# HGRN2's output norm on one Trainium2 core: 1/sqrt by logarithm and exponential on ScalarE in place of square roots and reciprocals

## The reference

```
def rmsnorm(x, g):
    xf = x.astype(jnp.float32)
    y = xf * lax.rsqrt(jnp.mean(xf * xf, axis=-1, keepdims=True) + RMS_EPS)
    return (y * g.astype(jnp.float32)).astype(x.dtype)
...
hg_o = hgrn2_chunked(qq, kk, g, vv)
hg_o = rmsnorm(hg_o, hg_norm_g).reshape(b, s, HG_VAL_WIDTH).astype(x.dtype)
u_hg = jnp.einsum('bse,ed->bsd', hg_o * jax.nn.silu(hg_z), w_hg_proj)
```

## Time and profile before

| | us |
|---|---|
| median of 3 runs (1442.77 to 1444.6) | 1443.66 |
| the profiled execution, its own time | 1442.67 |
| its span, first to last instruction | 1440.6 |
| TensorE matmuls busy | 1355.1 (94%) |
| VectorE busy | 959.2 (67%) |
| GpSimd busy | 709.6 (49%) |
| ScalarE busy | 577.1 (40%) |

### The profile page before, as it was taken

One profiled execution on the slowest core, in us unless ns is written; L12 is line 12 of the kernel. 1 busy time (PEld: TensorE's weight loads), 2 busy tenths in 40 slices (PEclk: granted clock), 3 DMA queues, 4 the chain that ended last, 5 costly groups with the idle time before them and its releaser, 6 DMA issues.

```text
span 1440.6 us, 23216 instructions
## 1 busy us (share of the span) xinstructions
PE 1355.1 (94%) x8408; PEld 1122.2 (78%) x8408; DVE 959.2 (67%) x1074; ACT 577.1 (40%) x958; POOL 709.6 (49%) x488
## 2 busy tenths in 40 slices
PE   5689999999999999999999999999898979999998
PEld 4568778778878878878878887887776768888886
DVE  4827976976977886896797697687533275545323
ACT  8336255346335535634634634543423321111131
POOL 6655744654565554564574465555556522223210
PEclk8799999999999999999999999999989989999999
DMA  5121121112111121121112111122343475433512
GB/s 147 29 74 30 60 86 32 61 45 71 62 30 59 46 74 59 30 89 59 30 61 73 45 61 45 58 74 89 103 158 105 151 241 177 154 95 116 192 44 102
DMA packets 134348, 119.41 MB, mean 83 GB/s; under 512 B 10096, under 2 KB 116592, under 8 KB 134256
## 3 DMA queue, kind: packets, MB, share of 16 engines
q1 hardware_dynamic: 125040, 92.84, 20.5%
q10 hardware_dynamic: 9216, 25.17, 5.1%
HBM read 88.63 MB, written 29.36 MB: 82 GB/s over the span
## 4 chain that ended last, share of the span: by engine, by line
PE 66%; DVE 12%; issue 9%; ACT 4%; POOL 4%; DMA 4%; SPq 0%; DVEq 0%; POOLq 0%; ACTq 0%
PE banks L1506 32%; PE banks L1756 12%; PE banks L1778 6%; PE banks L1584 4%; PE banks L1563 3%; DMA w_raw<-in_w_in 3%; DVE hk L1040 3%; PE banks L1574 2%; POOL b_lo L568 2%; POOL b_sum L568 2%; DVE forget L1040 1%; DVE hq L1040 1%; DVE scT L1272 1%; PE banks L1643 1%; DVE scT L1244 1%
## 5 line engine op out<-in xcount | busy, mean ns | idle before, releaser
L1506 PE MATMUL banks<-a_hi,b_hi 128*128 128x512 f32 x1120 | 468.4, 418 | 37.7 <-POOL b_lo L568 17.4
L1506 PE MATMUL banks<-a_hi,b_lo 128*128 128x512 f32 x1120 | 445.5, 398 | 0.0
L1506 PE MATMUL banks<-a_lo,b_hi 128*128 128x512 f32 x1120 | 444.5, 397 | 0.0
L568 POOL TENSOR_TENSOR b_lo<-w_raw,b_hi 128x512 fp32r<-128x512 f32 x120 | 183.0, 1533 | 300.8 <-ACT b_hi L656 291.7
L1506 PEld LDWEIGHTS banks<-a_hi,b_hi 128*128 128x128 f32 x1120 | 215.3, 192 | 86.2 <-POOL b_lo L568 19.9
L1506 PEld LDWEIGHTS banks<-a_hi,b_lo 128*128 128x128 f32 x1120 | 214.3, 191 | 48.1
L1506 PEld LDWEIGHTS banks<-a_lo,b_hi 128*128 128x128 f32 x1120 | 215.7, 193 | 37.5
L568 POOL TENSOR_TENSOR b_lo<-b_sum,b_hi 128x512 fp32r<-128x512 f32 x120 | 176.8, 1474 | 129.1 <-ACT b_hi L656 129.1
L1142 DVE TENSOR_TENSOR_SCAN kappa<-kappa 128x128 f32<-128x128 f32 (+3 forms) x64 | 97.0, 1516 | 100.8 <-ACT kappa L773 100.8
L656 ACT ACTIVATE b_hi<-b_sum 128x512 fp32r<-128x512 f32 x120 | 75.5, 631 | 136.9 <-POOL b_sum L568 136.9
L640 POOL TENSOR_TENSOR w_lo<-w_raw,w_hi 128x1024 fp32r<-128x1024 f32 x20 | 48.1, 2409 | 153.7 <-ACT w_hi L656 153.7
(11 more groups left out here) (194 smaller groups left out, 2467.7 us busy)
## 6 DMA issues: line engine op xcount, KB each, us to landing
w_raw<-in_w_in SPq DMA_DIRECT2D x80, 512.0 KB, 5.0
gate_d<-gate_out SPq DMA_DIRECT2D x16, 512.0 KB, 3.6
gate_in<-gate_d ACTq DMA_DIRECT2D x32, 256.0 KB, 2.9
x_tok<-in_x SPq DMA_DIRECT2D x8, 512.0 KB, 6.1
z_d<-z_out SPq DMA_DIRECT2D x8, 512.0 KB, 2.7
hz_d<-z_out SPq DMA_DIRECT2D x8, 512.0 KB, 2.7
osb_d<-o_sb SPq DMA_DIRECT2D x8, 512.0 KB, 5.7
ohg_d<-hq SPq DMA_DIRECT2D x8, 512.0 KB, 2.7
```

The lines of the kernel that those rows point to most:

```text
L568: return nc.gpsimd.tensor_tensor(dst, a, b, op)
L1506: last = mm(bank, w[:, s, k, :], t[s][:, k, :], start=opens and k == 0 and z == 0, stop=k == QUAD - 1 and z == 2, skip_group_check=not opens)
```

## The change

The square roots become logarithms, `log(mean + eps)`, still by halves; one exponential of the whole tile with the scale -0.5 gives `scT` = 1/sqrt; the four reciprocals and their semaphore go; `normalize` waits for the exponential, and the transposes of `turn_in` wait for the logarithms, which are now what reads `attended`.

```diff
-        def quarter(t, i):
-            return t[:, i * S // 4:(i + 1) * S // 4]
...
                 if u == 12:
                     act.wait_ge(hn_done, a + 1)
                     for b in range(2):
-                        nc.scalar.activation(halfs(scT, b), (turned, attended)[b], ACT.Sqrt, bias=EPS).then_inc(rms_done, 1)
+                        nc.scalar.activation(halfs(scT, b), (turned, attended)[b], ACT.Ln, bias=EPS).then_inc(log_done, 1)
+                    act.wait_ge(log_done, 2 * a + 2)
+                    nc.scalar.activation(scT[:, :], scT[:, :], ACT.Exp, scale=-0.5).then_inc(rms_done, 1)
...
-            def invert(a, i):
-                dve.wait_ge(rms_done, 2 * a + i // 2 + 1)
-                v.reciprocal(quarter(scT, i), quarter(scT, i)).then_inc(recip_done, 1)
-
             def normalize(a):
-                dve.wait_ge(recip_done, 4 * a + 4)
+                dve.wait_ge(rms_done, a + 1)
                 dve.wait_ge(on_done, 2 * a + 2)
                 tt(hq[:, :], hq[:, :], scT[:, :], ALU.mult).then_inc(hg_norm, 1)
...
                 take_c12(pairs[1], n + 1)
-                if attend:
-                    for i in range(3):
-                        invert(a, i)
                 take_c21(pairs[1], n + 1, h)
-                if attend:
-                    invert(a, 3)
...
             take_c12(GATE_PAIR, n)
-            for i in range(3):
-                invert(a, i)
             dve.wait_ge(gate_stored[0], 16)
             take_c21(GATE_PAIR, n)
-            invert(a, 3)
             normalize(a)
...
-                    need(pe, rms_done, 2 * h)
+                    need(pe, log_done, 2 * h)
```

More of the change, by code:

```diff
@@ L328, in build @@
         hn_done = sem("hn_done")
+        log_done = sem("log_done")
         rms_done = sem("rms_done")
-        recip_done = sem("recip_done")
         hg_norm = sem("hg_norm")
```

## The result

| | before | after |
|---|---|---|
| median, us | 1443.31 (16 runs, 1440.47 to 1444.9) | 1447.18 (16 runs, 1444.65 to 1449.03) |
| the profiled execution, its own time, us | 1442.67 | 1447.67 |
| its span, us | 1440.6 | 1445.9 |

The ratio is 1.0027 with a 95% interval of 1.0019 to 1.0034: slower by 3.9 us. The forecast was 1447.6, slower too.

A forecast was written before the change was run, and what follows sets the result against it. TensorE, busy 94% of the span, was taken to bound the kernel. Seven heads at +1.0 us (+7.0) and the gate stretch (-3.1) gave +3.9 on 1443.66, so 1447.6 us, range 1441.6 to 1451.4.

The forecast's parts named there:

- The second table load and the exponential: ScalarE in each head: a 1.28 us load and a 1.05 us exponential start the `b_hi` for P3 2.4 us later.
- rival 3: One table holds logarithm and exponential, no second load: -0.2 us a head, gate load 4.3 us earlier, -5.7, 1438.0 us; 6%.
- Turn-taking: Loop heads: VectorE's normalisation and scan delay GpSimd's `b_lo` and T4, whole instructions at a time; T4 ends at 327.97, undisturbed 327.24.
- rival 1: No turn-taking at the start of `b_lo` and T4: a head loses only 0.26 us, total -1.3, 1442.4 us; 20%.
- +1.0 us a head: Loop heads: TensorE's second group of transposes comes 1.0 us later in each, 7.0 us for the seven.
- The gate stretch, -3.1: Last head, among the gate pairs: the load of gate pair 3 goes out 3.1 us earlier; bounds nothing to 3.8.
- so an earlier load there is gained to the end: Gate pairs: load, split and load follow each other, so the whole 3.1 us of the earlier load was counted as gain.
- six waits for `b_lo`: Gate pairs: TensorE's waits for `b_lo`, counted as 17.4 us in six, taken as a sign of one chain.
- TensorE's first idle time in the gate pairs below 1 us: Sign that the forecast is right: TensorE's idle time of 3.78 us before gate pair 3 shrinks below 1 us.
- Rival 2: The gate stretch gives nothing back, the transfer or T4 of pair 2 coming late: +7.0, 1450.7 us; 12%.

The follow-up runs named there:

- e4: Changed kernel with ScalarE's exponential, and so its table load, moved behind the `b_hi` for P3, in the loop and the last head: 1435.65 us, ratio 0.9948.
- e6: Changed kernel with exp(-mean) in place of log(mean), so one table serves both functions and the second load goes; norm values differ: 1439.16 us, ratio 0.9971.
- e3: Changed kernel with VectorE's normalisation of `hq` moved behind its first scan: 1443.81 us, ratio to before 1.0000.
- e7: Changed kernel with VectorE's preparation of the first attention output moved ahead of `take_c22` in gate pair 2: 1445.71 us, ratio to before 1.0018.
- e2: Kernel before with the change in the last head (head 7) alone; the loop keeps roots and reciprocals: 1442.27 us, ratio 0.9991.
- e13: Changed kernel with four 128x1 reciprocals, into columns nobody reads, where the loop's four reciprocals stood: 1448.8 us, ratio to before 1.0044.
- e9: Kernel before with the weights load of gate pair 3 moved ahead of the two stores in SP's queue: 1440.01 us, ratio 0.9981.
- e5: Kernel before with all four reciprocals of the loop's heads moved behind `take_c21`: 1457.57 us, ratio 1.0105.
- e1: Kernel before with the change in the loop's seven heads alone; head 7 keeps roots and reciprocals: 1449.28 us, ratio 1.0042.
- e12: Kernel before with the loop's four reciprocals and the normalisation moved behind the first scan and its product: 1442.96 us, ratio 0.9999.

## Why the prediction held, and where it was off

- **The second table load and the exponential.** As forecast: two loads, 1.28 and 1.06 us, and the `b_hi` for P3 later by both. e4 and e6 show that this is the cause of the loss, by moving it and by halving it.
- **The table loads.** In e4 a function ends at 324.22 and the next load runs from 324.24 to 325.52. The drain that the Trainium skill adds to a load (ScalarE: Activation LUTs, "What ACT_TABLE_LOAD costs") isn't in these rows. The program has two loads around each norm where rival 3 had one; its condition wasn't met. The one load for both functions that the Trainium skill has (ScalarE: Activation LUTs, "Table sets: the hidden batching unit") isn't what this program has. e6, which has one load, took 1439.16 us, 3.8 below before, where the rival had 5.7; its parts are +0.1 us a head instead of -0.2, -2.3 in the gate stretch instead of -4.3, and -1.2 between heads and gates, which the rival didn't have.
- **Turn-taking.** As forecast in kind and size: `b_lo` 1.81 (1.79 in the sum), T4 drawn out by the scan. e3 shows it by taking it away; rival 1 falls for the kernel as it is.
- **+1.0 us a head.** Measured 1.0, with 1.65 us idle at the second group as forecast, and 7.1 us for seven. Taking the tail of the chain from head 0's rows, where the same chain ran late by itself, was what made this exact.
- **The gate stretch, -3.1.** Over-sized: -1.55 in the profile of after, of which 0.7 is steady (0.85 in the mean of the kernels). The load did leave 2.9 us earlier. The step that failed is the one from there to TensorE, "so an earlier load there is gained to the end": 0.8 us was lost until ScalarE had the weights, and then `b_lo` and `b_sum` came beside VectorE's work on the attention output, which they had missed before, 1.4 us (e7). What does reach TensorE's wait at gate pair 3 is kept: the stretch behind it is as long in all kernels, within 1.5 us. The prediction looked for such encounters in the head and not here. It also counted six waits for `b_lo` there; five are in the gate pairs (17.0 us), the sixth, of 0.45 us, is in head 0. "TensorE's first idle time in the gate pairs below 1 us" was wrong: 3.08. Rival 2 (nothing given back) falls, though by little: what speaks against it is the 0.85 us by which all kernels with the change in head 7 come earlier to pair 3's wait, more than the stretch of 1.55 or e2's median, 1.4.
- **Not foreseen, and it filled the gap:** 1.2 us between heads and gates. e13 shows that four short instructions more in VectorE's loop take them back, so the change does bring them, by another way than any term of the sum. The sum of the profiled parts without the start, 7.1 - 1.55 - 1.2 = +4.4, lies near the forecast's +3.9 partly by two errors that cancel: a gain of 1.55 us too much, and one of 1.2 us not counted. That the total came out to 0.4 us is luck in that part. With the steady 0.85 us in place of 1.55 the parts give +5.1, which is 1.2 more than measured and just above the interval of the ratio (2.7 to 4.9 us): the account of the parts closes to about 1 us and no better.

## What to carry to other kernels

An instruction moved off a busy engine onto an idle one is paid where the idle engine has something queued for the critical chain: place it behind that, and only then count the gain; here the same work cost 4 us or gave 8. When a step comes earlier or later, look again at what GpSimd and VectorE do at that moment, at every place it moves, not only the one under study. And where a queue holds a load behind a store, price an earlier load by all that stands between it and the engine that waits: here 2.9 us became 0.7 at TensorE, and 6.0 us became 1.7 (e9).

## What the runs showed of the hardware

- Where VectorE leaves the loop it is silent 3.2 us or 2.1 us, and four tiny instructions more or fewer in the loop decide which (all 14 kernels of this study, before and after among them). The releaser that the profile names there, a store, is not the cause.
- An idle time of 2.06 us inside a dense stream of matmuls was followed by 3.3 us at half the granted clock in every second head of e5 (0.52, 0.50, 0.50) and not in the others (1.00), with the same instructions: 1.6 us each.
- GpSimd's `TENSOR_TENSOR` and VectorE's `TENSOR_TENSOR_SCAN` (0.42 us alone) exclude each other as two `TENSOR_TENSOR` do: 1.10 and 1.50 us beside T4 in e3 and e6. VectorE's reciprocals, with one input, don't: in before T4 (323.57 to 324.85) lies wholly beside three of them and takes 1.28 us, and so in every head:

```profile
321.27 4.98 DVE L1272 RECIPROCAL scT<-scT 128x256 f32<-128x256 f32 x3 [1.16 <-ACT scT L804]
```

- The 1 MB of weights of gate pair 3 reached ScalarE's `b_hi` 6.5 to 7.2 us after the load's issue where that came 44.6 us behind the wait for `gate_out` (before, e1, e5, e12), and 7.4 to 7.5 us after it where it came at 41.6 (after, e2, e3, e4, e7, e13). Why the earlier load takes longer, no run here shows.
